# One matmul group re-ordered in a sliding-attention layer, two weight slots split earlier, one activation table fetched at the start

## The reference, cut to what matters

```
for l in range(2):
    h = swiglu(rmsnorm(x, g[0]), ...);            x = x + 0.5 * rmsnorm(h, g[1])
    h = mixer(rmsnorm(x, g[2]))                   # l = 0: mixer_even, l = 1: forgetting attention
    x = x + rmsnorm(h, g[3])
    h = swiglu(rmsnorm(x, g[4]), ...);            x = x + 0.5 * rmsnorm(h, g[5])

mixer_even(h):
    z = h @ w_in                                  # u, gate (512 each), q (8 heads x 64), k, v (2 x 64)
    a_out = silu(layernorm(causal_conv31(u * sigmoid(gate)) + b))
    b_out = sliding_window_attention(q, k, v)     # blocks of 128, window 128, ALiBi, a sink per head
    return concat(a_out, b_out) @ w_out
```

## Time and profile before

| | |
|---|---|
| median of 3 runs | 1645.89 us |
| the profiled execution | 1646.49 us, span of the trace 1644.6 us |
| TensorE (PE) busy | 1616.3 us, 98% |
| VectorE (DVE) busy | 1093.0 us, 66% |
| ScalarE (ACT) busy | 924.0 us, 56% |
| chain that ended last, by engine | PE 92%, DVE 4%, ACT 3%, issue 1% |
| DMA | 283.91 MB, mean 173 GB/s |
| mean granted TensorE clock | 0.997 of full |

### The profile page before, as it was taken

One profiled execution on the slowest core, in us unless ns is written; L12 is line 12 of the kernel. 1 busy time (PEld: TensorE's weight loads), 2 busy tenths in 40 slices (PEclk: granted clock), 3 DMA queues, 4 the chain that ended last, 5 costly groups with the idle time before them and its releaser, 6 DMA issues.

```text
span 1644.6 us, 23989 instructions
## 1 busy us (share of the span) xinstructions
PE 1616.3 (98%) x9475; PEld 1370.5 (83%) x9475; DVE 1093.0 (66%) x1727; ACT 924.0 (56%) x1557; POOL 42.3 (3%) x80
## 2 busy tenths in 40 slices
PE   8999999999999999999999999999999999999998
PEld 7887888878788888888886778888888889788887
DVE  5877776778558677665676465657656666675665
ACT  5755755566555555644576564546545565574544
POOL 3000000000020000000001000000000000000000
PEclk9999999999999999999999999999999999999999
DMA  8444676554265655656654256665565655456662
GB/s 285 136 146 128 198 228 201 185 163 153 65 202 178 195 179 174 210 181 192 190 162 128 75 169 200 183 193 179 184 200 179 195 180 153 129 167 192 183 190 76
DMA packets 210103, 283.91 MB, mean 173 GB/s; under 512 B 9585, under 2 KB 178819, under 8 KB 209993
## 3 DMA queue, kind: packets, MB, share of 16 engines
q1 hardware_dynamic: 208344, 278.42, 53.8%
q0 software_dynamic: 1648, 3.97, 0.7%
HBM read 281.15 MB, written 1.07 MB: 172 GB/s over the span
## 4 chain that ended last, share of the span: by engine, by line
PE 92%; DVE 4%; ACT 3%; issue 1%; DMA 0%; DVEq 0%; ACTq 0%
PE two L2100 84%; DVE w_lo L1383 1%; ACT w_hi L789 1%; PE two L2175 1%; PE two L2359 1%; PE two L2694 1%; PE two L2346 1%; PE two L2369 1%; PE two L2680 1%; PE two L2340 0%; PE two L2460 0%; ACT act_parts L836 0%; PE two L2161 0%; PE two L2372 0%; ACT p_sb L973 0%
## 5 line engine op out<-in xcount | busy, mean ns | idle before, releaser
L2100 PE MATMUL two<-act_parts,w_hi 128*128 128x512 f32 (+1 forms) x2784 | 801.7, 353 | 1.4 <-ACT act_parts L1165 1.4
L1383 DVE TENSOR_TENSOR w_lo<-raw,w_hi 128x1024 fp32r<-128x1024 f32 (+1 forms) x520 | 612.7, 1221 | 115.2 <-ACT w_hi L789 114.5
L2100 PE MATMUL two<-act_parts,w_lo 128*128 128x256 f32 x2256 | 635.0, 281 | 0.0
L2100 PEld LDWEIGHTS two<-act_parts,w_hi 128*128 128x128 f32 x2784 | 487.0, 188 | 83.0 <-issue 7.3
L789 ACT CAST w_hi<-raw 128x1024 fp32r<-128x1024 f32 (+1 forms) x520 | 516.4, 1050 | 4.4 <-DMA raw<-in_ffn_w_up 4.1
L2100 PEld LDWEIGHTS two<-act_parts,w_lo 128*128 128x128 f32 x2256 | 425.5, 189 | 2.1
L2100 PE MATMUL two<-w_hi,act_parts 128*128 128x512 f32 (+2 forms) x832 | 254.4, 383 | 8.1 <-DVE w_lo L1383 5.8
L914 ACT COPY p_sb<-two 128x512 f32<-128x512 f32 x108 | 62.6, 579 | 247.9 <-PE two L2100 247.9
L2100 PE MATMUL two<-w_hi,hid_even 128*128 128x512 f32 x576 | 189.3, 394 | 0.6
L2100 PEld LDWEIGHTS two<-w_hi,act_parts 128*128 128x128 f32 x832 | 153.4, 191 | 42.9 <-issue 8.0
L1509 DVE TENSOR_TENSOR pt_sb<-two,p_sb 128x512 f32<-128x512 f32 x54 | 37.3, 691 | 198.9 <-ACT p_sb L914 198.9
(11 more groups left out here) (318 smaller groups left out, 1223.0 us busy)
## 6 DMA issues: line engine op xcount, KB each, us to landing
raw<-in_ffn_w_up SPq DMA_DIRECT2D x160, 512.0 KB, 3.9
raw<-in_ffn_w_down SPq DMA_DIRECT2D x132, 512.0 KB, 3.5
raw<-in_ffn_w_gate SPq DMA_DIRECT2D x80, 512.0 KB, 3.7
raw<-in_a_w_in SPq DMA_DIRECT2D x24, 512.0 KB, 4.8
raw<-in_fox_w_in SPq DMA_DIRECT2D x20, 512.0 KB, 4.0
raw<-in_ffn_w_up SPq DMA_DIRECT2D x32, 256.0 KB, 3.4
raw<-in_w_kv SPq DMA_DIRECT2D x12, 512.0 KB, 3.6
raw<-in_mem_w_kv SPq DMA_DIRECT2D x8, 512.0 KB, 11.0
```

The lines of the kernel that those rows point to most:

```text
L1383: nc.vector.tensor_tensor(w_lo[:, r, 0:n], raw[:, r, 0:n], w_hi[:, r, 0:n], ALU.subtract).then_inc(lo_done, 1)
L2100: return nc.tensor.matmul(dst, a, w, start=start, stop=stop, skip_group_check=True)
```

## The change

1. **Start.** ScalarE's first work is now a fetch of the table of the square root, right after the first semaphore of GpSimd. Before, its first work was the copy at L1017.
2. **Splits ahead of a residual.** The `splits` in front of the residual of the even mixer goes to slot 294 and not 292, on ScalarE and VectorE. Slots 293 and 294 were split inside `arrive`: 293 behind the first token block's activations, 294 further on.
3. **Order on TensorE.** `turns("swa", 0)` moves from ahead of GU1's first token block to ahead of its chunk 3. The second pair's turn and the first pair's values move from chunk 4 to chunk 6. `stack(0, 0)` moves from chunk 6 to behind the projection.

```diff
@@ scalar
             act.wait_ge(ident_ready, 1)
+            fetch_table(ACT.Sqrt)
             for b in range(NTB):
@@ scalar
-            splits(292)
+            splits(294)
             arrive(EV["swa"], 3, ACT.Silu)
@@ tensor
             scores("swa", 0)
             scores("swa", 1)
             project("GU0", 1)
-            turns("swa", 0)
-            project("GU1", 0, {4: [lambda: turns("swa", 1), lambda: values("swa", 0)], 6: [lambda: stack(0, 0)]})
+            project("GU1", 0, {3: [lambda: turns("swa", 0)], 6: [lambda: turns("swa", 1), lambda: values("swa", 0)]})
+            stack(0, 0)
             scores("swa", 2)
             values("swa", 1)
             stack(0, 1)
```

## The result

The changed kernel took 1636.10 us (median of 5 runs, 1635.68 to 1637.20). The kernel before, run beside it, took 1645.32 us. The ratio is 0.9942, with a 95% interval of 0.9930 to 0.9955. The direction is as forecast. The time lies 0.2 us under the low end of the range (1636.3). The profiled execution took 1635.79 us with a span of 1633.8.

A forecast was written before the change was run, and what follows sets the result against it. TensorE, busy 98% of the span, was taken as the bound, so only its stands and slow clock could be won. 0.4 + 3.0 + 5.0 = 8.4 us off the median 1645.89 gave 1637.5, range 1636.3 to 1640.3.

The forecast's parts named there:

- Part 1: Start: early table fetch lets the first copy move until the first weight slot's landing limits it; 0.4 us, bounds 0 to 1.28.
- Part 2: GU1: ready matmuls shrink the 3.09 us stand to 1.0, clock stays full, new 0.8 us wait at third scores; 3.0 us.
- Part 3: Network 3's first projection: earlier splits remove a 3.17 us stand and the slow clock after it; 5.0 us.
- The cover: Residual ahead of network 3: x of block 0 is ready 2.5 us before TensorE transposes it, absorbing lateness.
- The sum: Whole kernel: gains at the start, in GU1 and in network 3 add to 8.4 us.
- (a): GU1: the new order gives little, as the clock still drops or the scores' wait adds; 1639.2 to 1640.1 us, chance 0.14.
- (b): Network 3: a wait for block 1's x or activations replaces the stand, clock still drops; 1639.3 to 1641.0 us, chance 0.09.
- (d): Both stands: something other than what was moved ends them, only the start's gain remains; 1645.5 us, chance 0.03.
- (e): Residual: slot 294 lands late and ScalarE and VectorE stand; slower than before, 1649.6 us at a 19 us load, chance 0.02.
- (c): Start: TensorE reaches full clock earlier, 1.3 us instead of 0.4; 1636.6 us, chance 0.06 with other small gains below that.
- the step from the gain to a time and its range: Whole kernel: the gain taken off the median 1645.89 gives 1637.5 us, range 1636.3 to 1640.3.
- the price of a stand: TensorE after each of the two long stands: about 1.7 us lost at the lower clock, 1.2 GHz.

The follow-up runs named there:

- e5: The changed kernel once more, unedited: 1637.14 us (5 runs), ratio 0.9953 to the kernel before.
- e16: The changed kernel plus 11 and 12 identity transposes keeping TensorE busy at the start, run again in a later job: 1636.16 us, ratio 0.9942 to the kernel before.
- e13: The changed kernel without the early fetch of the square root's table: 1637.13 us, ratio 0.9950 to the kernel before.
- e2_order: The kernel before with only the new order in GU1 on TensorE: 1643.33 us, ratio 0.9985.
- e3: The kernel before with only the splits up to 294 ahead of the residual: 1640.51 us, ratio 0.9967.
- e12: The changed kernel with the splits ahead of the residual up to 295 in place of 294: 1636.66 us, ratio 0.9951 to the kernel before.
- e7: The changed kernel with the splits ahead of the residual up to 296 in place of 294: 1644.28 us, ratio 0.9999 to the kernel before.
- e4: The kernel before once more, unedited: 1646.05 us (11 runs), ratio 1.0005 to itself in the same job.
- e10: The kernel before plus 11 and 12 identity transposes keeping TensorE busy at the start, no early fetch: 1644.63 us, ratio 0.9998.
- e9_best: The changed kernel with a second order in GU1 (turns, values, stacks and third scores moved) and 11 and 12 identity transposes at the start: 1634.21 us, ratio 0.9936.
- e11: The kernel before with the early table fetch and 11 and 12 identity transposes on TensorE at the start: 1643.76 us, ratio 0.9992.
- e1: The kernel before with only the early fetch of the square root's table: 1645.16 us, ratio 0.9996.
- e6: The changed kernel plus 11 and 12 identity transposes keeping TensorE busy at the start: 1636.40 us, ratio 0.9948 to the kernel before.
- e8: The changed kernel with another order in GU1 (first turn at chunk 5, second turn at chunk 7): 1635.56 us, ratio 0.9944 to the kernel before.

## Why the prediction was right or wrong

**Part 1, the start: right in size as far as can be told, though the profile pair seemed to say otherwise.** Forecast 0.4 us; at equal clock -0.2 to 0.43 us in three pairs of traces, 0.3 over all ten, and 0.3 to 0.5 by the medians, within their noise. The mechanism was as described: the first slot's landing took the place of the table load. The landing was given as 7.52. It came between 7.1 and 8.1 in the profiles with the fetch, so the first matmul lay between 9.56 (e5) and 10.56 (e16). Not foreseen: TensorE waits another 0.4 to 0.7 us for slot 2 when it runs at full clock, as in the changed kernel (0.66 us at 13.32). I had written that every later slot is ready before it is needed, which held for the low clock only. And the bounds of 0 to 1.28 took the start's clock as given; with the same first matmul at 10.41 it moved the end of the projection by 2.1 us (before to e13).

**Part 2, the order in GU1: right.** Forecast 3.0 us; the pair of profiles gives 895.86 - 890.20 = 5.66, less 2.67 from ahead of it, so 3.0, and e2_order alone 2.5 by its ratio. The stand of 1.0, the clock at 1.00 after it, and the new wait of 0.8 us at the third scores are all there.

**Part 3, the splits: right.** Forecast 5.0 us; 5.09 in the pair, 5.05 in e3's profile against before, 5.4 by e3's ratio. ScalarE was 0.5 us ahead (0.3 forecast). The cover behind that, 2.5 us forecast, measured 2.9 in e12 and 3.5 in e7, and e7 shows the price beyond it.

**The sum: right against many executions.** 8.4 us were forecast. All runs of the kernel before in the five jobs, e4's among them, have a median of 1645.31 (93 runs), all runs of the changed kernel 1636.85 (15 runs): 8.5 us. The jobs of the experiments ran on different chips. The single parts sum to 8.6. Rivals (a), (b), (d) and (e) did not occur; (c), the start's clock, did in the profiled execution, with 2.5 us instead of its 1.3, but not by the fetch: e13 shows the full clock without it.

**What failed: the step from the gain to a time and its range.** The prediction put it as "the gain is the same for both ... and the median 1637.5". The 8.4 us were taken off 1645.89, a median of three runs, and the range went only 1.2 us below. The base term was mis-sized: over 93 runs it is 1645.31, 0.6 us less. The changed kernel's own five runs lay 0.75 us under its pooled median, a lucky draw. With the gain 0.06 us over the forecast these make up the 1.4 us from 1637.5 to 1636.10. From the pooled base the same gain gives 1636.9, and a low end as far below would be 1635.7, under the measured time. The kernel before scatters over 8 us (1641.8 to 1649.7), which three runs within 0.85 us did not show. I gave the range no share for either. I bounded what the edits cost, as if the base had no error.

Two places of the scatter are shown: the clock behind long stands, which made the same stretch 1.0 us longer in e10 than in before, and the start's clock (24.38 in e3 and 23.07 in e4, 1.3 us apart with the same instructions there). They don't add up to 8 us; that the rest is the clock too is supported only by the mean clocks of the 88 executions. I took 1.7 as the price of a stand. It is one draw: in five executions there was none, and a gain near 8.4 holds for the middle of the executions and not for each. From 1641.9, the middle of those five, to the changed kernel's 1636.85 it is 5 us.

**A better version.** e9_best, the second order and the busy start, took 1634.21 us, 2.6 us less than the changed kernel's pooled median in other jobs and 2.5 less than e12 in its own, and beats both kernels (ratio 0.9936 to the kernel before). I expected 2.2. Its waits of TensorE have nothing at the first turn nor at the third scores, and 0.8 us as the longest for a weight split, at the start.

## What to carry to other kernels

Where TensorE carries the chain, look for its few long stands and fill them with matmuls that are ready, or take away the one split they wait for; in the profiles each of the two here paid back about one and a half times what was taken from it (3.0 us for 2.1, and 5.1 for 3.2), because the clock no longer fell. In executions where the clock does not fall anyway, only the length is won. After such a walk through queues, check the next waiter: `o_lo` behind a moved stack gave back 0.8 us, and could be read from the order beforehand. And take the base from many executions before a narrow range is set around it: a kernel with long stands can scatter by far more than three runs show, and one pair of profiles can credit a small edit with 2 us of luck.

## What the runs showed of the hardware

- Behind a stand of 3.1 to 3.2 us the granted clock fell to 0.50 in all seven profiles that have one. Its windows lose 1.7 us in most and 3.4 us in e10 and e11, and there the stretch was 1.0 us longer. In five of 88 executions of the kernel before the mean clock leaves no room for a fall. After stands of 1.0, 0.8 and 1.6 us it did not fall in any profile here.
- Kernels with both stands scattered by 5 to 6.6 us between executions (e1, e4, e10, e11, and the kernel before in the jobs of the experiments), those with neither by 0.7 to 2.6 (after, e5, e6, e8, e9, e12 to e16). Part of this is the count of runs, 9 to 28 against 5 or 6, but the standard deviations differ too: 1.6 us for the kernel before (93 runs), 0.8 for the changed kernel (15). With one stand left it was 5.1 (e2, 11 runs) and 2.7 (e3, 6 runs).
- At the start the clock can be low or full for the same program. Where it is low from the first matmul, the granted clock of the windows doesn't show it (before reads 1.00 from 8 to 16), but the distance of the matmuls does: 0.43 us against 0.23. Where it falls after a few matmuls, as in e8, the windows do (0.50 from 12 to 15).
- The first 512 KB slot landed 5.4 to 6.4 us after its issue in otherwise equal starts.
